# One vector instruction moved in the second unit of each seven-product block: the lower sum ahead of the next unit's weight sums

## The reference

```python
def _swiglu(h, w_in, w_out):
    a, b = jnp.split(h @ w_in, 2, axis=-1)
    return (jax.nn.silu(a) * b) @ w_out

x = x + MACARON_SCALE * _swiglu(_rmsnorm(x, ln_ffn1[i]), ffn1_w_in[i], ffn1_w_out[i])
```

## Time and profile before

| what | value |
|---|---|
| median of three runs | 2186.64 us (2186.15 to 2188.95) |
| profiled execution, its own time | 2188.33 us |
| span of its profile | 2186.6 us |
| TensorE (PE) busy | 2142.7 us, 98% |
| VectorE (DVE) busy | 1600.6 us, 73% |
| ScalarE (ACT) busy | 906.9 us, 41% |
| mean granted TensorE clock | 0.995 of full speed |

### The profile page before, as it was taken

How to read it: one execution, slowest core, us unless ns; L and a number is a source line. 1 busy time by engine, 2 the same in 40 slices (tenths; PEclk the granted TensorE clock), 3 DMA queues, 4 the chain that set the end, 5 groups by cost and what they waited for, 6 DMA issues and landing times.

```text
span 2186.6 us, 42987 instructions
## 1 busy us (share of the span) xinstructions
PE 2142.7 (98%) x17360; PEld 2108.6 (96%) x17360; DVE 1600.6 (73%) x2462; ACT 906.9 (41%) x1284; POOL 5.7 (0%) x19
## 2 busy tenths in 40 slices
PE   9999999999999989999999999999989999999998
PEld 8999999999999889999999999999988999999998
DVE  5766776457878789778487887848797579686774
ACT  5222232234545455445155543515533345253443
POOL 0000000000000000000000000000000000000000
PEclk9999999999999999999999999999999999999999
DMA  5233543243242144445245242424374434242332
GB/s 142 77 90 105 161 128 108 73 116 80 60 117 60 52 117 113 129 125 146 63 128 138 68 124 85 142 64 116 109 218 149 108 91 124 84 137 87 97 88 81
DMA packets 439814, 234.91 MB, mean 107 GB/s; under 512 B 34849, under 2 KB 432370, under 8 KB 439666
## 3 DMA queue, kind: packets, MB, share of 16 engines
q1 hardware_dynamic: 426562, 218.76, 35.5%
q10 hardware_dynamic: 12528, 13.08, 1.8%
q0 software_dynamic: 576, 1.05, 0.3%
HBM read 212.67 MB, written 23.30 MB: 108 GB/s over the span
## 4 chain that ended last, share of the span: by engine, by line
PE 93%; DVE 5%; issue 1%; DMA 1%; ACT 1%; SPq 0%; DVEq 0%; ACTq 0%
PE ps L2519 52%; PE ps L2631 33%; PE ps L2748 2%; PE ps L2482 1%; PE ps L2938 1%; PE ps L2927 1%; PE ps L2913 0%; PE ps L2826 0%; DVE w_lo L1500 0%; DVE o_rs L2243 0%; DMA w_raw<-in_ffn_w_in_dram 0%; DMA wb<-wb_d 0%; PE ps L2790 0%; PE ps L2799 0%; PE ps L2817 0%
## 5 line engine op out<-in xcount | busy, mean ns | idle before, releaser
L2631 PE MATMUL ps<-hf_hi,s_hi 128*128 128x288 f32 x1848 | 547.6, 296 | 9.6 <-issue 4.5
L2631 PE MATMUL ps<-hf_lo,s_hi 128*128 128x288 f32 x1848 | 543.2, 294 | 0.0
L2631 PE MATMUL ps<-hf_hi,s_lo 128*128 128x288 f32 x1848 | 542.5, 294 | 0.0
L2631 PEld LDWEIGHTS ps<-hf_hi,s_hi 128*128 128x128 f32 x1848 | 346.9, 188 | 12.6 <-issue 7.2
L2631 PEld LDWEIGHTS ps<-hf_lo,s_hi 128*128 128x128 f32 x1848 | 347.2, 188 | 0.2
L2631 PEld LDWEIGHTS ps<-hf_hi,s_lo 128*128 128x128 f32 x1848 | 346.9, 188 | 0.0
L1588 DVE TENSOR_TENSOR s_lo<-s_raw,s_hi 128x1024 fp32r<-128x1024 f32 (+1 forms) x264 | 286.5, 1089 | 60.6 <-ACT s_hi L987 52.9
L987 ACT ACTIVATE s_hi<-s_raw 128x1024 fp32r<-128x1024 f32 (+1 forms) x264 | 250.2, 950 | 191.5 <-PE ps L2631 183.2
L929 ACT ACTIVATE w_hi<-w_raw 128x1024 fp32r<-128x1024 f32 (+4 forms) x141 | 185.7, 1323 | 242.4 <-PE ps L2519 239.4
L2519 PE MATMUL ps<-h_hi,w_hi 128*128 128x288 f32 x1216 | 267.8, 302 | 2.2 <-issue 1.1
L2519 PE MATMUL ps<-h_hi,w_lo 128*128 128x288 f32 x1216 | 260.5, 296 | 0.0
(11 more groups left out here) (415 smaller groups left out, 3081.1 us busy)
## 6 DMA issues: line engine op xcount, KB each, us to landing
s_raw<-in_ffn_w_in_dram SPq DMA_DIRECT2D x330, 256.0 KB, 3.3
w_raw<-in_ffn_w_out_dram SPq DMA_DIRECT2D x96, 256.0 KB, 3.2
w_raw<-in_ffn_w_in_dram SPq DMA_DIRECT2D x44, 512.0 KB, 5.1
w_raw<-in_hgrn_w_in_dram SPq DMA_DIRECT2D x32, 512.0 KB, 5.4
w_raw<-in_ffn_w_out_dram SPq DMA_DIRECT2D x48, 192.0 KB, 2.6
w_raw<-in_s_w_glu_dram SPq DMA_DIRECT2D x16, 512.0 KB, 5.1
w_raw<-in_ffn_w_out_dram SPq DMA_DIRECT2D x16, 384.0 KB, 4.0
w_raw<-in_ffn_w_out_dram SPq DMA_DIRECT2D x16, 320.0 KB, 3.7
```

The costliest lines, as they stand in the source:

```text
L2631: ins = M.matmul(out, w, h, start=f in (0, 1, 3) and k == 0 and n == 0, stop=f in (3, 5, 6) and k == KP - 1 and n == 2, skip_group_check=True)
```

## The change

In the second unit of each fast block (`v % UNITS == 1`) the lower sum is issued directly behind the first unit's gate, where before it came behind the next unit's three weight sums, the low half of the gated result and the first low half of the next unit's weights. Since it writes `fc22`, which the gate reads, it now also waits for the gate's own signal `g_full`. Other units are untouched, and so are the other engines' programs.

```diff
                     if vl:
                         gate(vl - 1)
+                    if v % UNITS == 1:
+                        dve.wait_ge(g_full, base + vl)
+                        lower_sum(v)
                     if nxt is not None:
                         sum_three(nxt)
                     if vl:
                         gate_rest(vl - 1)
                     if nxt is not None:
                         unit_rest(nxt, 0)
-                    if v % UNITS == 1:
-                        lower_sum(v)
                     if nxt is not None:
                         sum_fourth(nxt)
                         unit_rest(nxt, 1)
```

## The result

The changed kernel is slower: 2192.31 us median of nine runs (2190.45 to 2197.38) against 2187.94 us of nine runs of the kernel before, ratio 1.0024, 95% interval 1.0015 to 1.0033. Three later timings of the same program gave 1.0027 (1.0015 to 1.0038), 1.0032 (1.0021 to 1.0043) and 1.0029 (1.0013 to 1.0046). The ratio lies closer to that of the means of the runs, 2193.1 and 2187.7 us, 5.5 us apart, than to that of the medians, 4.4 us apart. The profiled execution took 2190.45 us with a span of 2188.7.

The account below looks back on a forecast made before the run. DVE was taken to bound the stretch up to the third unit's lower sum, so its added idle time is lost: +1.80 + 1.01 + 1.00 = +3.8 us on 2186.64 gives 2190.4 us, range 2186.0 to 2192.5.

Parts of the forecast that it names:

- the 4.9 us of lateness: Second unit's p6, held by the lower sum: 1.11, 1.90 and 1.90 us late in the three blocks, all to go.
- The wake of the lower sum: Delay from p5's start to the moved lower sum's start on DVE: bounded by 0.20 and 0.28 us, taken as 0.27.
- DVE's idle time: DVE idle behind the first unit's gate until p4 is done: about 1.7, 0.9 and 0.9 us in the three blocks.
- The pauses: New TensorE pauses in the third unit: about 1.3 us before p0 and 1.7 us before p2 (first block).
- That nothing comes back: Rival: TensorE saves its 4.4 us of waiting for the lower sum, giving 2182.2 us; chance 0.05.
- That only the third unit's start counts: Rival: only p0's wait for the first low half matters; sum -1.2 us, 2185.4 us; chance 0.12.
- That the change does not act: Rival: p4's signal comes so late that p6 still waits; time about that of the forecast; chance 0.02.
- The clock: Rival: TensorE's third-unit pauses lower its clock for two products per block, 9.4 us more, 2199.9 us; chance 0.03.
- the step from the sum to "same": Whole program: +3.6 to +4.1 lies just inside "same", 2182.3 to 2191.0 us; same 0.67, slower 0.27, faster 0.06.
- The sum of +3.6 to +4.1 us: Three blocks' loss together: +3.6 with wake 0.20 us, +4.1 if restarting costs 0.1 us per block; forecast +3.8.
- the stated range: Whole program's time was predicted to lie between 2186.0 and 2192.5 us.
- Every later start moves with it: Behind the third unit's p6 TensorE has no pause to absorb the shift, so all later starts shift equally.

Follow-up runs that it names:

- the run whose pause was 2.7 us: Kernel before, with DVE waiting for p4 of the second unit directly behind the gate and the lower sum at its old place: ratio 1.0026.
- the last experiment: Kernel before, with the lower sum behind the weight sums (second unit) or ahead of `sum_fourth` (third, fourth), ACT's snapshots reordered: 2183.04 us, ratio 0.9978.

## Why the prediction was wrong

The mechanism in the blocks was right, step by step. p6 of the second unit starts when due, and the 4.9 us of lateness go. The wake of the lower sum was put at 0.27 us and is 851.36 - 851.10 = 0.26. DVE's idle time was forecast as about 1.7, 0.9 and 0.9 us and is 1.70, 0.90 and 0.91. The blocks were to lose 1.80, 1.01 and 1.00 us and lose 1.79, 0.99 and 0.99. The pauses were put at the right two places, with the lateness about right: p0 1.2 us late (855.47 - 852.67 - 1.58) for 1.3, p2 1.8 (860.42 - 855.47 - 3.18) for 1.7.

The rivals fell. That nothing comes back is refuted by the blocks, which got slower instead of faster by 4.4 us in all. That only the third unit's start counts asked for +0.13 and -0.67 us a block, and +1.79 and +0.99 came. That the change does not act is refuted by p6 of the second unit, which follows p5 by 1.57 us in all three blocks. The clock did not fall in the blocks of the changed kernel. It did in the run whose pause was 2.7 us, so that rival named a real price, but the pauses of 1.05 and 1.52 us did not bring it.

What failed is the step from the sum to "same", which got 0.67. It rests on the sentence that "a measurement of this kernel tells about 0.2% from no change, 4.4 us", for which the prediction gives no row or run, and that term was mis-sized. Nine runs a side gave the ratio as 1.0015 to 1.0033, 0.0009 either way, which is 2 us. The sum of +3.6 to +4.1 us is 1.0016 to 1.0019. It lies within what was measured and is clear of 1.000 by nearly twice that, so the prediction's own mechanism and numbers asked for "slower". The place to which the sum was added was off as well: the median of three runs, 2186.64, is 2187.94 over nine, and three runs from 2186.15 to 2188.95 did not show a scatter that reaches 2198.85 in later runs of the same kernel. That 2192.31 lies in the stated range is partly luck: the three later timings of the changed kernel have medians of 2193.39, 2195.42 and 2197.27 us.

A second term was put at nothing on thin ground. "Every later start moves with it" is read from 31 us of one block, and 6.1 us, the mean of the four timings, is more than the blocks' 3.8. But the runs do not show this step to have failed. The profiles of the changed kernel have +1.45 us in the S5 mixer on the mean, but two kernels that are delayed as much or more stay within the range of the kernel before there, and kernels with unchanged blocks were timed 1.5 to 2.4 us over too. The cause stays open.

## What to carry to other kernels

A wait of the busiest engine is worth only what the chain behind it lets through: look whether the engine that it waits for is idle anywhere between this wait and the next one it ends. If it is not, removing the wait alone moves it, and an idle time put in to remove it is lost in full. Only where the order behind it was changed too did these waits give time back (5.3 us in the last experiment). And before a forecast says "no change", work out from the scatter of the runs what their number can tell apart, here 2 us. A step that must wait belongs at the first place in the queue where its signal has already come, not at the first place where it may stand; behind the weight sums it cost the blocks nothing.

## What the runs showed of the hardware

- A single TensorE pause of 2.7 us was followed by some 5 us at a granted clock of 0.69, 0.67 and 0.66 in the three blocks, while a pause of 1.7 us, or two of 1.05 and 1.52 us a few us apart, left it at 1.00.
- An execution can stop TensorE for 4.9 us at a loop's next pass with no semaphore to blame; in the one profile that caught it, the instruction queue moved 110 packets where it moved 100 in the profile before the change, two of them inside the pause. That the packets are the cause is not shown.
- DVE went on 0.20 us behind the start of p5 where p4's signal was the first of three that the row names in the code, and 0.26 us behind it where it was the second of three, in all three blocks each time.
- Stretches bound by engine order repeat to 0.03 us from one execution to the next, while the whole program scatters by 3 to 13 us: comparing the same matmuls of two profiles resolved 0.02 us where the intervals of five rounds of timing are 2 to 4 us either way. The last matmul is no end mark: it came 0.76 us later in its stretch on the mean, and the program ended as much sooner behind it.
